# A hybrid decoder step on eight cores: row norms moved ahead of state copies, sample transposes put off, one dependency per block in the last part

## The reference

```python
n = rmsnorm(x, norm_mix_g); proj = n @ w_in
cb, cc, ch, q, k, v, g, a_lr, gate_a, gate_b = jnp.split(proj, SPLIT_POINTS, axis=-1)
uc, conv_new = causal_dwconv(cc * ch, conv_prev, conv_mix_w)      # mixer A
y_a = (cb * uc) @ w_conv_out
logg = jax.nn.log_sigmoid((a_lr @ w_gate_up + b_gate)) / 16       # mixer B: gated linear attention
# per token: S = diag(exp(logg)) S + k^T v ; o = q S   (4 heads, 256 x 512 state)
o = rmsnorm(o, gla_norm_g); y_b = (o * silu(g)) @ w_gla_out
h = x + (sigmoid(gate_a) * y_a + sigmoid(gate_b) * y_b) @ w_o
a, gt = jnp.split(rmsnorm(h, norm_ffn_g) @ w_ffn_up, 2, axis=-1)  # ConvFFN
gc, ffn_new = causal_dwconv(gt, ffn_prev, ffn_conv_w)
y = rmsnorm(h + (silu(gc + ffn_conv_b) * a) @ w_ffn_down, final_norm_g)
```

## Time and profile before

| | |
|---|---|
| median of 3 runs | 2745.86 us |
| lowest and highest | 2722.34 and 2887.11 us |
| profiled execution | 2723.86 us; span of its slowest core 2722.3 us |
| spans of the 8 cores | 2714.3 to 2722.3 us, granted clock 0.986 to 0.989 |
| PE busy | 2563.8 us (94%), 14552 products |
| DVE busy | 1023.6 us (38%) |
| ACT busy | 722.0 us (27%) |

### The profile page before, as it was taken

How to read it: one execution, slowest core, us unless ns; L and a number is a source line. 1 busy time by engine, 2 the same in 40 slices (tenths; PEclk the granted TensorE clock), 3 DMA queues, 4 the chain that set the end, 5 groups by cost and what they waited for, 6 DMA issues and landing times.

```text
span 2722.3 us, 39115 instructions; the slowest of 8 cores (2714.3 to 2722.3 us)
## 1 busy us (share of the span) xinstructions
PE 2563.8 (94%) x14552; PEld 1386.1 (51%) x14552; DVE 1023.6 (38%) x1994; ACT 722.0 (27%) x1401; POOL 151.3 (6%) x289
## 2 busy tenths in 40 slices
PE   5989998988888999999999999999999999999994
PEld 2345454544444555555555445555455545554552
DVE  4462223342425453322112225444244423442355
ACT  3443233433332111221110134332022202320232
POOL 0000000000000000000000000000000000000000
PEclk9989999999999999999999999999999999999997
DMA  7251252625343677676443533342443244433533
GB/s 194 45 161 39 39 124 65 161 55 126 76 103 87 155 170 171 155 164 171 79 69 65 128 57 68 64 69 53 75 83 67 52 73 83 71 58 58 90 72 139
DMA packets 85938, 261.01 MB, mean 96 GB/s; under 512 B 7956, under 2 KB 9620, under 8 KB 82278
## 3 DMA queue, kind: packets, MB, share of 16 engines
q0 software_dynamic: 41040, 148.98, 33.0%
q1 hardware_dynamic: 44712, 109.53, 12.0%
HBM read 361.45 MB, written 45.99 MB: 150 GB/s over the span
## 4 chain that ended last, share of the span: by engine, by line
PE 89%; DVE 4%; ACT 3%; issue 2%; DMA 1%; SPq 0%; DVEq 0%; ACTq 0%
PE ps L335 87%; PE ps L338 2%; DVE a_og L361 1%; DMA a_xb<-xp 1%; DVE a_z L351 1%; DVE a_z L361 1%; ACT a_Sbf L348 0%; ACT a_junk L348 0%; ACT a_xno L348 0%; DMA a_xb<-xo 0%; ACT L348 0%; ACT a_og L348 0%; DVE a_uc L361 0%; DVE a_U L361 0%; DVE a_npT L351 0%
## 5 line engine op out<-in xcount | busy, mean ns | idle before, releaser
L335 PE MATMUL ps<-a_nT,ring 128*128 128x385 bf16 (+4 forms) x4224 | 712.0, 328 | 0.3
L335 PE MATMUL ps<-a_n2T,ring 128*128 128x384 bf16 (+1 forms) x4224 | 689.2, 325 | 0.0
L335 PEld LDWEIGHTS ps<-a_nT,ring 128*128 128x128 bf16 x4224 | 414.7, 98 | 289.1 <-issue 6.5
L335 PEld LDWEIGHTS ps<-a_n2T,ring 128*128 128x128 bf16 x4224 | 409.5, 97 | 278.5 <-issue 0.3
L335 PE MATMUL ps<-ring,a_actb 128*128 128x512 bf16 x1584 | 342.8, 379 | 4.5 <-DVE a_z L351 4.5
L376 POOL DMA_DIRECT2D ring<-wflat x284 | 150.4, 530 | 2479.2 <-PE ps L335 1467.5
L335 PEld LDWEIGHTS ps<-ring,a_actb 128*128 128x128 bf16 x1584 | 154.8, 98 | 191.5 <-issue 5.6
L351 DVE TENSOR_TENSOR a_z<-a_z,ps 128x512 f32<-128x512 f32 x180 | 123.0, 686 | 301.3 <-PE ps L335 284.4
L361 DVE SCALAR_TENSOR_TENSOR a_gc<-a_gte,sb_sb_cst,a_gc 128x383 f32<-128x383 f32 (+3 forms) x352 | 182.4, 518 | 36.7
L355 DVE TENSOR_SCALAR a_gc<-a_gte,sb_sb_cst 128x383 f32<-128x383 f32 (+3 forms) x176 | 64.7, 367 | 335.4 <-ACT a_gte L348 330.4
L361 DVE SCALAR_TENSOR_TENSOR a_S<-a_S,a_dls,ps 128x512 f32<-128x512 f32 x128 | 95.5, 746 | 252.1 <-PE ps L335 241.2
(11 more groups left out here) (138 smaller groups left out, 1773.8 us busy)
## 6 DMA issues: line engine op xcount, KB each, us to landing
ring<-wflat POOLq DMA_DIRECT2D x284, 512.0 KB, 5.7
a_S<-sgla SPq DMA_DIRECT2D x64, 512.0 KB, 6.2
o_glas<-a_S SPq DMA_DIRECT2D x64, 512.0 KB, 3.6
a_xb<-xo SPq DMA_DIRECT2D x9, 1024.0 KB, 5.9
a_z<-xo SPq DMA_DIRECT2D x9, 1024.0 KB, 16.4
y<-a_z SPq DMA_DIRECT2D x18, 512.0 KB, 3.0
a_xb<-xp SPq DMA_DIRECT2D x8, 1024.0 KB, 19.4
o_glap<-a_U SPq DMA_DIRECT2D x4, 512.0 KB, 2.8
```

The source lines that it names most:

```text
L335: P.op("pe", lambda e: e.matmul(out, lhsT=lhsT, rhs=rhs, start=start, stop=stop), reads=r, writes=w)
```

## The change

Five edits. The fifth prefix tile's `pre1` moves from before the transposes of the fourth tile into `aux[0]`, behind unit 0. In `chain_step`, `ep_a` moves ahead of the copies to `Sbf`, and `ep_og` from the start of the next step to the end of its own. The transposes of a head's sample rows are put off to the fourth `smp_tick` that follows (`smp_ep`). The transposes of `stl` move from the start of P4 behind the first block of its groups. In the last down part `z` has one key per tile and column block.

```diff
     pre1(0)
     for i_ in range(4):
-        pre1(i_ + 1)
+        if i_ < 3:
+            pre1(i_ + 1)
         pre2(i_, 0)
         pre2(i_, 1)
...
-    aux = {0: [lambda: pre1(5), lambda: pre2(4, 0)], 1: [lambda: pre2(4, 1)],
+    aux = {0: [lambda: pre1(4), lambda: pre1(5), lambda: pre2(4, 0)], 1: [lambda: pre2(4, 1)],
...
-    smp = {"n": 0, "ready": 0, "loaded": 0}
+    smp = {"n": 0, "ready": 0, "loaded": 0, "ep": None}
+
+    def smp_ep(force=False):
+        if smp["ep"] is None:
+            return
+        h, k = smp["ep"]
+        if k > 0 and not force:
+            smp["ep"] = (h, k - 1)
+            return
+        ep_b(h, NPO, 128, 1)
+        smp["ep"] = None
...
         if s == 15:
             ep_a(128, BS, 1)
             ep_og(128, BS, 1)
-            ep_b(h, NPO, 128, 1)
+            smp["ep"] = (h, 3)
...
     def smp_tick(rate):
+        smp_ep()
         acc["v"] += rate
...
     def chain_step(h, ci):
         nch = len(CH_OWN)
-        if 1 <= ci <= nch:
-            t0, n = CH_OWN[ci - 1]
-            ep_og(n, BO, 0)
         if ci < nch:
...
                 stt(U[:, dk, :], U[:, dk, :], sc, ps[:, BP[dk], :], ALU.mult, ALU.add,
                     [("U", dk), ("dl", h % 2), PSB(BP[dk])], [("U", dk)])
+            ep_a(n, BO, 0)
             for dk in range(2):
                 dst, kd_ = (Sbf, ("Sbf", dk)) if ci < nch - 1 else (U, ("U", dk))
                 act(dst[:, dk, :], U[:, dk, :], AF.Copy, [("U", dk), ("dl", h % 2)], [kd_],
                     scale=dl[h % 2][:, dk, ci:ci + 1])
-            ep_a(n, BO, 0)
+            ep_og(n, BO, 0)
...
     dma(stl[:, :], sconv, None, w=["stl"])
-    for c in range(8):
-        tr(ps[:, BT, c * 32:(c + 1) * 32], stl[0:32, c * 128:(c + 1) * 128], identf[0:32, 0:32],
-           ["stl", "identf"], [PSB(BT)])
-    cp(sprev_u[:], ps[:, BT, 0:256].rearrange("p (c s) -> p c s", c=8), [PSB(BT)], ["sprev_u"])
...
         prefetch()
+        if c2 == 0:
+            for c in range(8):
+                tr(ps[:, BT, c * 32:(c + 1) * 32], stl[0:32, c * 128:(c + 1) * 128], identf[0:32, 0:32],
+                   ["stl", "identf"], [PSB(BT)])
+            cp(sprev_u[:], ps[:, BT, 0:256].rearrange("p (c s) -> p c s", c=8), [PSB(BT)], ["sprev_u"])
...
     while smp["n"] < 64:
         smp_step()
+    smp_ep(True)
...
-        tt(zs, zs, ps[:, bank, :], ALU.add, [("z", ti), PSB(bank)], [("z", ti)])
-        if last:
-            act(junk[:, :], zs, AF.Square, [("z", ti)], ["junk", ("st8", ti)], accum=st8[:, ti, g:g + 1])
+        if not last:
+            tt(zs, zs, ps[:, bank, :], ALU.add, [("z", ti), PSB(bank)], [("z", ti)])
+            return
+        tt(zs, zs, ps[:, bank, :], ALU.add, [("z", ti), PSB(bank)], [("zb", ti, g)])
+        act(junk[:, :], zs, AF.Square, [("zb", ti, g)], ["junk", ("st8", ti)], accum=st8[:, ti, g:g + 1])
...
             stt(zs, zs, st8[:, ti, 6:7], gfin[:, hf * 1024:(hf + 1) * 1024], ALU.mult, ALU.mult,
-                [("z", ti), ("st8d", ti), "gfin"], [("z", ti), ("zf", ti, hf)])
+                [("zb", ti, 2 * hf), ("zb", ti, 2 * hf + 1), ("st8d", ti), "gfin"], [("zf", ti, hf)])
```

## The result

| | before | after |
|---|---|---|
| median | 2727.3 us | 2633.7 us |
| lowest to highest, runs | 2724.8 to 2746.3, 10 | 2629.6 to 2635.9, 4 |
| profiled: span, granted clock of all cores | 2722.3, 0.986 to 0.989 | 2634.4, 0.988 to 0.992 |

The ratio of the two is 0.966 (95% interval 0.963 to 0.968). The column of before holds ten later runs, made beside the last experiments; the three that stood ahead of the prediction are not in it. The spans differ by 87.9 us, where 81.9 were forecast.

What follows compares the result with a forecast made beforehand. TensorE, busy in 94% of the span, was taken as the bound, so only its waits and lower-clock time could be won. 47.6 + 1.5 + 18.5 + 6.6 + 11.8 - 4.1 = 81.9 us off 2723.9 gave 2642 us, range 2618 to 2688.

Steps and rivals of the forecast that it cites:

- chain, with clock: Chain steps of four heads: waits for `a_og` go, step 5.33 to 4.1 us; 47.6 us won, plus 1.5 of clock.
- sample rows: Sample rows of each head: all 15.4 us of waits go, with clock 18.5 us won (15 to 18.5).
- stl: Transposes of `stl` at P4's start: the 4.31 us wait and lower clock behind it go; 6.6 us won (4.3 to 6.6).
- tail: Last part, seven output tiles: adds no longer wait for squares, period 8.03 to 6.35 us; 11.8 us won (8 to 13.6).
- start: Fifth tile's norm now directly ahead of its transposes: 3.9 us wait, 1.5 clock, 1.3 gained; 4.1 us lost net.
- The first step: First chain step in three of four heads, with a table load of 1.28 us: 0.7 us of wait kept each, 2.1 together.
- handed on: First rival, chain: state products wait for late copies instead; half of each wait stays, 25 us, 2665 us; chance 0.13.
- The second: Rival: delay at the start reaches PE, loss of 10 us, 2648 us; chance 0.16 together with the third.
- The third: Rival: sample rows and tail held by something else, such as banks; 8 us each, 2656 us; chance 0.16 with the second.
- The fourth, the clock: Rival: denser chain and tail lower the clock in every run, 165 us slower, 2807 us; chance 0.05.

Runs made afterwards that it cites:

- u_sample: The changed kernel with the transposes of a head's sample rows right behind their norm again, the other edits kept: 2655.3 us.
- u_stl: The changed kernel with the eight transposes of the convolution's sample state back at the start of P4, right behind their load: 2644.8 us.
- s_mid: The changed kernel with the fifth prefix tile's norm behind the fourth tile's norm and transposes, ahead of the logits and decays: 2627.3 us.
- u_chain: The changed kernel with both moves of the chain edit (`ep_a` and `ep_og`) undone, the four other edits kept: 2692.6 us.
- u_tail: The changed kernel with the old whole-tile keys of `z` in the last part: 2647.1 us.
- u_start: The changed kernel with the first half of the fifth prefix tile's norm in its old place again: 2630.2 us.
- t_junk2: s_mid with the tail squares' dump tile and accumulator dependency also split: 2622.5 us, ratio 0.961 to the kernel before.
- d_nostore: t_junk2 without the 16 stores of the first head's sample states: 2622.7 and 2627.0 us.

## Where the prediction held, and the step of it that failed

The step that failed is a size: "Without the wait a step takes 4.1 us", and from it "So the step of 5.33 us becomes one of 4.1." It became 3.95, and the term of the chain, 47.6 + 1.5 = 49.1 us, measured 55.0. The second term that was off is the tail's.

| term | forecast | between the two profiles | undone alone |
|---|---|---|---|
| chain, with clock | 49.1 | 55.0 | 59 |
| sample rows | 18.5 | 15.3 | 21 |
| `stl` | 6.6 | 6.7 | 11 |
| tail | 11.8 | 14.8 | 13 |
| start | -4.1 | -4.0 | -4 (-6 in the middle place) |

The third column adds up to 87.9 but for rounding, 6.0 more than the forecast; the other 2 of the 8 us by which the median is lower are the profiled run's place above it. It is read at landmarks inside the mixed stretches. Up to the first update product of head 3's chain (800.83 us before, 753.43 after) 7.7 us are won, less 1.0 for the eight `stl` transposes, which come later now. From 858.78 (795.29 after) on 2.8 are won by the second head's sample rows, and what lies between, 17.0, is the last head's chain. The first head's sample rows are the 5.7 won ahead of head 2's chain. The last column adds up to 98 to 100 where 93.6 were won. Most of that surplus is not the edits': 2.1 us of `u_sample`'s stand ahead of P3, and in `u_stl` the transfer took 1.8 longer and another wait 1.2.

- **The chain step.** I took the wait of 1.23 off, let PE be ready at 404.87 - 1.23 = 403.64, and read the 4.10 of the earlier trace rows as PE's work. But 403.64 is the modelled end of the two products ahead of the wait. Timeline of PE, these products before and after:

```profile
403.05 0.59 PE L335 MATMUL ps<-a_vto,a_kT 128*128 128x512 bf16 x2
```

```profile
404.58 0.59 PE L335 MATMUL ps<-a_vto,a_kT 128*128 128x512 bf16 x2
```

Both show 0.59 us, but after the change the transposes start 0.44 behind their start (405.02). Before they started 1.82 behind (404.87). So 1.38 us could be won per step, and the bracket shows 0.15 less. The eight steps of the first head took 42.51 us before and 31.11 now, 11.4 less, where the waits in them add up to 10.1. In the three heads of P3 this is 3.8 us more than forecast. Another 0.7 come from their first steps: their waits of 1.70, 1.63 and 1.63 were to shrink to 0.7 each and shrank to about 0.5. The last head gave 17.0 us, forecast 15.6 (waits of 14.1 and 1.5 of clock). The order of events was as forecast: square to exponential beside the DVE updates, `ep_og` at 403.64 and the copies at 403.44, both ahead of PE.
- **The first step** was to keep 0.7 us in three heads; it keeps 0.53, 0.46 and 0.46. The load of the table takes 1.28 us again (394.30) and the next activation starts at 395.60, right behind it. So the drain of about 1380 ns that the Trainium skill gives ("ScalarE: Activation LUTs", What ACT_TABLE_LOAD costs) isn't seen in this trace either.
- **The sample rows**: all four waits went. The next head's first state product waits 2.14 us for its copy instead of 1.52, and the 16 products behind it took 3.74 us, where 48 of the same kind take 8.00 (2.67 for 16), so part of them ran at the lower clock; that head gave 5.7 us, not 7.8. I had costed what comes behind the old place at nothing. The last two heads gave 6.8, not 8.1. With this edit alone undone, 18.9 us come between P3's first product and PE's last, which is the forecast's 18.5.
- **`stl`**: as forecast, 6.7 us for 6.6; a wait of 0.21 us is left.
- **The tail**: the third square starts 2.40 us after the first add, forecast 2.41. What I had said "doesn't change" did: the two long operations and the way to the next add take 2.40 us, and took 2.60 before (2662.39 to 2664.99), since the second no longer waits for the first, which had written the same key. The other 0.13 of a period is a slip of the reading: the 4.09 comes from a tile of 7.90 us (2657.09 to 2664.99), and I took it off the mean of 8.03. 7 x 2.02 = 14.1.
- **The start**: the wait was forecast at 3.9 and is 4.24. The clock behind it cost 3.9 us, not 1.5: (2.07 - 1.12) + (6.15 - 3.63) + (1.01 - 0.61), against the same runs of `s_mid`. Behind it PE is 8.6 us late (68.33 against 59.77). That the profiles still differ by only 4.0 at P3's first product is luck: 3 us of the rest come back at 171 us, where PE waited 4.59 us before and 1.45 after for a tile of the core's own rows. The kernel before got there at 200.88 us, but the five other profiles without the late norm have it at 193.2 to 198.1 and seven with it at 201.9 to 206.9 (`u_chain`, with a granted clock of 0.980, is left out): 8.7 us between the means. Part comes back at the waits for state loads, which leaves the 4 to 6 of the medians.
- **Rivals.** The waits were not handed on to `a_Sbf`, which is not in PE's list. The second held in kind: the start costs 4 to 6 us, not the 10 of its upper end. The third fell with `u_sample` and `u_tail`. The fourth, the clock, fell too: from 1700 to 2600 us the granted clock is 1.00 as before, and all eight cores have 0.988 to 0.992 over their spans. The Trainium skill ("TensorE: Matmul & The Clock Gate", the note on the peak-current limiter) would have them at 13/16; this trace disagrees again.

So direction, places and mechanisms held. What was off is the size of two periods, the step's and the tail's, both worked out from stretches in which engines waited for each other. The two gave 8.9 us more than forecast and the sample rows 3.2 less; that the sum is off by only 6 is in part luck.

## What to carry to other kernels

Where a step waits, look for every in-order queue that holds the late instruction back; with two of them each edit alone showed about a quarter or less of what both gave here. Take a step's length without the wait from starts of products that follow each other without one, not from the busy time beside the wait. Work that is put off until right ahead of its user has to be moved to where both its old queue and its user have room: the middle place won what the late one lost.

## What the runs showed of the hardware that I had not expected

A wait of PE of a few us costs clock or doesn't, for no reason that the order shows. At one place of P1 the kernels wait 2.45 us for `a_npT` with the same products ahead of it, and 16 like products follow. Timeline of PE, `u_start` first, then `s_mid`:

```profile
89.57 3.61 PE L335 MATMUL ps<-a_npT,sb_sb_alrw 128*16 128x512 bf16 x16 [2.45 <-DVE a_npT L351]
```

```profile
89.44 6.51 PE L335 MATMUL ps<-a_npT,sb_sb_alrw 128*16 128x512 bf16 x16 [2.45 <-DVE a_npT L351]
```

In `t_junk2`, which has the same program there as `s_mid`, they take 4.93, in the kernel before 6.50. The mean granted clock over these products is 1.00 in `u_start`, 0.55 in `s_mid`, 0.73 in `t_junk2` and 0.55 before, so the slower ones ran mostly or partly at 1.2 GHz. A wait of this length costs between its own length and 3 us more. At the start the same program in two executions (the changed kernel, 204.86 and 201.91 us at P3's first product) differs by 3 us. The state loads of 512 KB issued from 440 to 525 us land in 3.4 us (median; 6.4 at most) in `d_nostore`, where the DMA engines are 66% busy from 480 to 520, and in 6.4 (12.7 at most) in `s_mid`, where they are 92% busy.
